# Two transformer layers moved ahead of a diffusion block, with the modulation weights loaded between their dense tiles

## The reference

```python
x = first_block(x, mem, ...)      # layer 0: sink attention + spatial gating unit + cross attention + 16 experts
                                  # layer 1: pooling mixer + cross attention + 16 experts
for i in range(2):                # second_block; last = (i == 1)
    mod  = silu(c)     @ ada_w[i] + ada_b[i]     # sh1, sc1, g1, sh2, sc2, g2 of the latents
    modc = silu(c_ctx) @ ada_w[i] + ada_b[i]     # the same six of the context
    h  = modulate(rmsnorm(x,  norm1_g[i]), sh1, sc1)
    hc = modulate(rmsnorm(xc, norm1_g[i]), csh1, csc1)
    y, yc = diff_attention(h, hc, ...) if i == 0 else gqa_attention(h, hc, ...)   # keys: context and latents
    x = x + g1 * y
    x = x + g2 * swiglu(modulate(rmsnorm(x, norm2_g[i]), sh2, sc2), ffn_w_gu[i], ffn_w_down[i])
    if not last:                  # the context gets its own output only in layer 0
        xc = xc + cg1 * yc
        xc = xc + cg2 * swiglu(modulate(rmsnorm(xc, norm2_g[i]), csh2, csc2), ...)
```

## Time and profile before

| | |
|---|---|
| time, median of 3 runs | 2428.16 us (2425.42 to 2431.86) |
| the profiled execution | 2427.91 us, of which its span 2426.1 us |
| busy in the span | PE 82%, PEld 62%, POOL 41%, DVE 31%, ACT 30% |
| granted clock of TensorE, mean | 0.909 of full speed |
| DMA | 482 MB, mean 199 GB/s |

### The profile page before, as it was taken

One profiled execution on the slowest core, in us unless ns is written; L12 is line 12 of the kernel. 1 busy time (PEld: TensorE's weight loads), 2 busy tenths in 40 slices (PEclk: granted clock), 3 DMA queues, 4 the chain that ended last, 5 costly groups with the idle time before them and its releaser, 6 DMA issues. The chain is left out here.

```text
span 2426.1 us, 29349 instructions
## 1 busy us (share of the span) xinstructions
PE 1992.6 (82%) x11525; PEld 1505.0 (62%) x11525; DVE 754.8 (31%) x1394; ACT 736.7 (30%) x1025; POOL 1003.2 (41%) x784
## 2 busy tenths in 40 slices
PE   5569579998779779996798699976975999787998
PEld 0029469987558644443687444435744999656997
DVE  0113832125443321113232311123784211453112
ACT  0024534443323210002233110012463444354442
POOL 0037048886227200003574000014703788524886
PEclk8879779999769989998999799997987999898999
DMA  8985236655214449997443399994402466312663
GB/s 328 374 290 172 70 108 181 184 191 182 78 52 156 157 174 409 409 409 281 138 160 119 115 410 409 409 366 156 128 12 78 146 186 192 123 52 79 190 180 99
DMA packets 298434, 482.25 MB, mean 199 GB/s; under 512 B 16890, under 2 KB 200172, under 8 KB 297932
## 3 DMA queue, kind: packets, MB, share of 16 engines
q1 hardware_dynamic: 288284, 458.67, 53.4%
q10 hardware_dynamic: 10032, 21.93, 2.7%
HBM read 476.77 MB, written 3.77 MB: 198 GB/s over the span
## 5 line engine op out<-in xcount | busy, mean ns | idle before, releaser
L580 POOL TENSOR_TENSOR w_lo<-raw,w_hi 128x512 fp32r<-128x512 f32 x780 | 1003.0, 1321 | 1404.7 <-ACT w_hi L1276 1404.6
L630 PE MATMUL PS<-at_hi,w_hi 128*128 128x256 f32 x1680 | 492.1, 293 | 33.0 <-DVE at_lo L1786 29.1
L1276 ACT ACTIVATE w_hi<-raw 128x2048 fp32r<-128x2048 f32 x195 | 371.6, 1909 | 384.5 <-PE PS L632 361.0
L631 PE MATMUL PS<-at_lo,w_hi 128*128 128x256 f32 x1680 | 484.5, 288 | 0.0
L632 PE MATMUL PS<-at_hi,w_lo 128*128 128x256 f32 x1680 | 484.3, 288 | 0.0
L630 PEld LDWEIGHTS PS<-at_hi,w_hi 128*128 128x128 f32 x1680 | 332.2, 198 | 41.5 <-DVE at_lo L1786 31.3
L631 PEld LDWEIGHTS PS<-at_lo,w_hi 128*128 128x128 f32 x1680 | 332.0, 198 | 4.2 <-issue 3.1
L632 PEld LDWEIGHTS PS<-at_hi,w_lo 128*128 128x128 f32 x1680 | 331.6, 197 | 0.0
L630 PE MATMUL PS<-w_hi,at_hi 128*128 128x512 f32 (+1 forms) x480 | 192.3, 401 | 56.4 <-DVE at_lo L1786 28.9
L631 PE MATMUL PS<-w_lo,at_hi 128*128 128x512 f32 (+1 forms) x480 | 188.9, 394 | 0.0
L632 PE MATMUL PS<-w_hi,at_lo 128*128 128x512 f32 (+1 forms) x480 | 188.5, 393 | 0.0
(11 more groups left out here) (296 smaller groups left out, 2369.9 us busy)
## 6 DMA issues: line engine op xcount, KB each, us to landing
raw<-ffn_w_gu SPq DMA_DIRECT2D x132, 512.0 KB, 4.9
raw<-ada_w SPq DMA_DIRECT2D x64, 768.0 KB, 6.4
raw<-l_e_gate SPq DMA_DIRECT2D x80, 512.0 KB, 10.8
raw<-ffn_w_down SPq DMA_DIRECT2D x66, 512.0 KB, 4.0
raw<-l_e_up SPq DMA_DIRECT2D x64, 512.0 KB, 8.2
raw<-diff_w_in SPq DMA_DIRECT2D x48, 512.0 KB, 4.7
raw<-l_e_down SPq DMA_DIRECT2D x48, 512.0 KB, 13.8
H<-l_e_down SPq DMA_DIRECT2D x40, 512.0 KB, 12.6
```

The costliest lines, as they stand in the source:

```text
L580: ins = nc.gpsimd.tensor_tensor(w_lo[:, n % RING, part], raw[:, n % RAW, part], w_hi[:, n % RING, part].bitcast(F32), ALU.subtract)
L630: pe.matmul(dst, s_hi, m_hi, start=first, stop=False)
L631: pe.matmul(dst, s_hi, m_lo, start=False, stop=False)
L1276: nc.scalar.activation(w_hi[:, n % RING, :], raw[:, n % RAW, :], ACT.Copy).then_inc(hi_done, 1)
```

## The change

The order becomes: (3) and (4) first, then (2) and the first half of (5) together, then the rest of (5). Three things change with it.

*The modulation* is no longer a stage. Its 64 tiles take slots of `raw` between the 27 dense tiles of layer 0, by two tables: `ADA_BEFORE[n]` is how many of them SP has loaded before dense tile n, `ADA_USED[n]` how many PE has used before it. Further ones are used in the attention loops of layer 0 (`mods(11 + it)` in each step of the first). Both conditionings and both layers now sum up in one bank (bank 7), so the other rotating banks are three instead of four until the experts of layer 0. A tile is loaded by two DMAs of 64 partitions. Memory is written before the experts of layer 0 and read behind them.

*The context* stays on the chip: its rows lie in the second half of `H` (`HC`), its keys and values of the differential attention are not written out.

*Context and latents* take turns in one function, `context_and_latents`, on PE, ACT and DVE, one on `at`, the other on `at2`.

```diff
+ADA_BEFORE = [0, 0, 0, 0, 2, 4, 5, 6, 8, 10, 14, 18, 22, 26, 36, 38, 40, 42, 44, 46, 48, 50, 52, 56, 57, 59, 64, MODS]
+ADA_USED = [0, 0, 0, 0, 3, 5, 7, 12, 16, 20, 24, 34, 36, 38, 40, 42, 44, 46, 48, 52, 54, 55, 56, 62, 63, 64, 64, MODS]
...
+            def slot_wait(s):
+                if RAW <= s < RAW + len(SEQUENCE):
+                    kind, at = SEQUENCE[s - RAW]
+                    sp.wait_ge(ada_used if kind == "ada" else lo_done, at + 1)
...
-            modulation(0, 0, RAW)
+            sp.dma_start(X[:, :, :], A["x"][0].rearrange("(t p) d -> p t d", p=P)).then_inc(input_landed, 16)
+            gemm(A["l0_w_in"], 0, D)
             for dst, src in loads[N_COLIN:]:
                 sp.dma_start(dst, src, allow_slow_non_contiguous=True).then_inc(setup_landed, 16)
-            sp.dma_start(X[:, :, :], A["ctx_2"][0].rearrange("(t p) d -> p t d", p=P)).then_inc(x_landed, 16)
-            modulation(0, RAW, MOD_TILES)
-            modulation(1, 0, MOD_TILES)
...
             def tile_wait():
+                mods(ADA_USED[min(c.get("tile"), LAYER_TILES[0])])
                 pe.wait_ge(lo_done, c.lo(c.get("tile")))
...
+            def context_and_latents():            # PE
+                gemm(2, at=1)                      # context V
+                to_at(HL, wait=False)              # latents
+                heads_t(4, 4, 0, False, at=1)      # context K, Q
+                diff_attention(0)
+                pe.wait_ge(y_freed, c.get("y"))
+                at_wait()
+                gemm(1)                            # latents V, first half
+                to_at(HC, wait=False)              # context behind its attention
+                gemm(1)                            # latents V, second half
+                at_wait()
+                gemm(1, at=1)                      # context output, first half
+                tables(0)
+                gemm(1, at=1)                      # context output, second half
+                heads_t(4, 0, 0, True)             # latents K
+                to_at(rows_q, wait=False)          # context, RMS
+                heads_t(0, 4, 0, True)             # latents Q
+                diff_attention(1)
+                gated(F_FFN // P, at=1, between=HL)   # context feed-forward, latents transposed in it
+                gemm(1)                            # latents output, first half
+                to_at(V[:, 2:4, :], wait=False)    # context, RMS
+                gemm(1)                            # latents output, second half
+                at_wait()
+                gemm(1, 256, at=1)                 # context V of the second attention
+                heads_t(1, 0, 1, False, at=1)      # and its K
+                to_at(HL)                          # latents, RMS
+                gated(F_FFN // P)                  # latents feed-forward
...
                 else:
                     to_at(X)
-                    gemm(2)
+                    columns()                      # the read-back modulation, transposed
+                    gemm(1)
+                    to_at(HL, wait=False)          # context, for its V, K, Q
+                    gemm(1)
```

More of the change, by code:

```diff
@@ L372, in build @@
         bias = A["ada_b_2"].rearrange("l (g n w) -> l n g w", g=4, n=3)
-        for layer in range(2):
-            for _, n, rows in mod_parts:
-                loads.append((mod_sums[layer][rows, :], bias[layer, n]))
+        for layer, _, n, rows in mod_parts:
+            loads.append((mod_sums[rows, :], bias[layer, n]))
         assert len(loads) == N_COLIN + N_SETUP
@@ L460, in moe @@
                 g, u, dw = (A[f"l{layer}_e_{s}"] for s in ("gate", "up", "down"))
-                dense, landed = c.get("tile"), layer * (MOE_TILES // MOE_RING)
+                mods_until(MODS)
+                dense = c.get("tile")
                 at = 0
@@ L603, in _, with mods @@
             c = Count()
+            def mods(end):
+                if 0 == c.get("ada") < end:
+                    pe.wait_ge(wb_freed, 7)
+                while c.get("ada") < end:
+                    a = c.get("ada")
+                    s = ADA_AT[a]
+                    pe.wait_ge(raw_landed[s % RAW], 32 * (s // RAW + 1))
+                    for n in range(3):
+                        ins = pe.matmul(mod_bank[32 * n:32 * n + 16, :], spread_of(a),
+                                        raw[:, s % RAW, n * 512:(n + 1) * 512], start=a == 0, stop=a == MODS - 1)
+                    ins.then_inc(ada_used, 1)
+                    c.add("ada")
             def tile_wait():
+                mods(ADA_USED[min(c.get("tile"), LAYER_TILES[0])])
                 pe.wait_ge(lo_done, c.lo(c.get("tile")))
@@ L764, in gated @@
                 step(True)
+                if between is not None:
+                    to_at(between, wait=False)
                 with pe.Fori(0, loops) as i:
@@ L840, in modulation @@
[L840 to L858, removed]
-            bank = wb_wait()
-            for wide in range(2):
-                ins = pe.matmul(bank[:, 2 * wide:2 * wide + 2], swap[wide][:, :], gains[:, 0, 2 * wide:2 * wide + 2],
-                                start=True, stop=True)
@@ L1378, in gated @@
                 step()
+                if between:
+                    to_at()
                 with act.Fori(0, loops) as i:
@@ L2071, in gated @@
                     step()
-                if early:
-                    dve.wait_ge(x_landed, 32)
-                    for _ in range(NT):
-                        ready(dve.tensor_copy(hs[:, 0, 0:1], hs[:, 0, 0:1]))
-                    to_at()
                 c.add("tile")
@@ L2153, in _ @@
             D1(dve.tensor_reduce(select[:, P:P + 4], ident[:, :].rearrange("p (r g) -> p g r", g=4), AXX, ALU.add))
+            full()
+            freed(dve.tensor_copy(col[:, :], bank()[:, 0:C_ROWS]))
+            dve.wait_ge(input_landed, 16)
+            for _ in range(NT):
+                ready(dve.tensor_copy(hs[:, 0, 0:1], hs[:, 0, 0:1]))
+            to_at()
             for wide in range(2):
```

545 lines of the change are left out of this document (281 added, 264 removed).

## The result

The changed kernel takes **2340.1 us** (median of 4 runs, 2337.9 to 2347.2), beside 2429.6 of the kernel before on the same chip: a ratio of 0.9639, 95% interval 0.9613 to 0.9664. The forecast was 2279, its range 2238 to 2322. The sign is right, the gain is 89 us where 148 were forecast.

What follows compares the result with a forecast made beforehand. PE was taken to set the pace outside the experts and a load-bound first stage of 164.6 us. Terms -144.6 + 40.6 + 8 - 52.2 = -148.2 took the span from 2426.1 to 2277.9; forecast 2279 us, range 2238 to 2322.

Steps and rivals of the forecast that it cites:

- Step 1: Start of the kernel: first dense product at 20 us (bounds 17 and 26) instead of 164.6, -144.6 us.
- Step 2: Modulation tiles put among layer 0's dense tiles and attention loops cost PE time: +40.6 us.
- rival E: Whole kernel: nothing gained, the modulation's 50 MB only displace other loads in layer 0; chance 0.02, including mixtures near no change.
- Dense tiles 7.5 us apart: Expected profile sign in layer 0: dense tiles of `w_out` and `xkv` 7.5 us apart, PE not waiting for `w_lo`.
- Step 3: Layer 1: reading the modulation back, small transposes, context transposes and a copy or two, +8 us (3 to 14).
- Step 4: Context and latents taking turns on the engines fill PE's gaps: -52.2 us (bounds -92 and 0).
- four stretches: Experts to context's K -18 us; context attention to output product -12; to latents' Q -7.6; to latents' feed-forward -14.6.
- The doubt about DVE beside POOL: Two head norms: DVE operations with two SBUF inputs wait for POOL's splits, sum about 8 us higher.
- C: Covers leak: ten DVE chains slowed by POOL, dense tiles late among modulation; +46 us, 2325 us, chance 0.18.
- Its sign: What would show the forecast wrong: sum of DVE waits above 60 us where context and latents take turns.
- D: Ring of four slots runs in series, 17.6 us a dense tile instead of 7.5: +232, 2511 us, chance 0.03.

Runs made afterwards that it cites:

- e4: Changed kernel without any load or slot for modulation tiles, products in full on a constant tile: 2268.7 us.
- e9: Changed kernel, modulation tiles keep slots and waits but load 128 of 1536 columns, products in full on a constant tile: 2288.9 us.
- e1: Changed kernel with each modulation tile loaded as two column halves over all 128 partitions instead of two halves of 64 partitions: 2308.1 us.
- e3: Changed kernel with all loads, but products of 62 of 64 modulation tiles over 16 columns instead of 512: 2335.0 us.
- e6: Changed kernel with ACT splitting the fourth dense tile of the context's V in layer 1 ahead of the latents' squares: 2333.4 us.
- e12: Kernel before the change, each modulation tile loaded as two column halves over 128 partitions instead of one transfer: 2430.0 us, ratio 1.0011.
- e2: Kernel before the change, with each modulation tile loaded as two halves of 64 partitions: 2514.3 us in a single run.

## Why the prediction was wrong

Added up, layer 0 by its windows: 311.3 without modulation, + 26.6 products (e4), + 20.6 order (e9, 358.5), + 21.1 bytes (e1, 379.6), + 33.0 partition halves = 412.6. The medians say much the same: 2239.8, 2268.7, 2288.9, 2308.1, 2340.1. The terms are differences in this order of taking things off; in another order the shares can differ (with late loads the products cost 5 us in e3, without loads 29 in e5).

- **Step 1** was right in mechanism, off by 4.7 us: PE's first dense product came at 24.7 instead of 20, inside its bounds of 17 and 26. ACT's third split ended at 20.7 where the prediction had 16; it waited for its tile.
- **Step 2 failed, at the sentence "The loads keep up by order: a dense tile's slot is freed by a modulation tile used three dense tiles earlier, 3 x 7.5 = 22 us, and load plus split need 12."** The prediction costed what TensorE issues, and took a load at the 4.7 us of the earlier trace rows, measured in a layer that moved 121 GB/s. Three prices are missing from it. They come to 75 us. The products were 12.7 cheaper, 1.3 of lateness was in the forecast already, and the rest of layer 0 took 3.5 more, which leaves the 64.
  - *Partition halves, 33 us.* The prediction gave the halves no term. It compared GB/s with GB/s in rival E (150 more would fit), while the load itself had become 1.7 times as dear in engine time.
  - *Bytes, 21 us.* Even in column halves the engines are at 0.65 in layer 0 (e1), and a dense tile of `l_xkv` took 6.2 us to land, where it took 4.7 in the quiet layer of the earlier trace rows and 4.3 in e4 at a share of 0.32.
  - *Order, 21 us.* The 22 us of slack hold for `w_out` to `xq`, where e9 and e4 differ by nothing. At both ends they don't: the first modulation tiles can't be used before the table is spread, and in the cross attention a dense tile queued behind modulation tiles holds ACT. The prediction had 2 us for the first and none for the second.
  - *Products, 27 us*, where 22.6 + 5 + 3 and the 8.7 of `w_in` make 39: more of them hides than was thought.
- **Dense tiles 7.5 us apart**: true of the first two distances only. The eight dense tiles between the gating unit and the transposes start at 212.4, 219.9, 227.4, 237.6, 248.3, 257.1, 269.4 and 278.8 us; PE waits for modulation tiles in between, not for `w_lo`, as was said. In e4 the same stretch is 66.6 us long instead of 79.6.
- **Step 3** was right to a microsecond. **Step 4** was right to a microsecond in its sum (-51.7 for -52.2), and that was luck: of its four stretches three missed by 6 to 8 us, in both directions. The windows of the changed kernel:

```profile
1201.20:1244.10 42.90, 27.58 (x113) 21.93 (x113) 26.68 (x39) 16.62 (x21) 37.01 (x27) 0.91 0.53 172
1345.50:1395.30 49.80, 46.12 (x214) 38.08 (x213) 25.18 (x31) 17.77 (x15) 37.24 (x29) 1.00 0.46 148
1395.30:1475.30 80.00, 67.06 (x456) 59.64 (x456) 48.07 (x50) 34.02 (x46) 42.92 (x33) 0.89 0.38 116
1538.90:1798.30 259.40, 232.90 (x1563) 215.73 (x1562) 89.97 (x119) 112.98 (x131) 201.56 (x156) 0.96 0.53 162
```

  The forecast had 37.2, 57, 72 and 261.5 us. The first stretch lacks the 6.3 us before the context's K. In the second the four half products took 11.0 to 11.2 us each at a clock of 1.00, not 11.5, the 16 transposes 1.9 instead of 3.7, and the head norm was covered to the end. In the third K and Q took 64.6 us, not 59, and 15.4 lie between them, not 13. The fourth was 2 us shorter than forecast. The experts, the context's K and Q and the two attentions, at 0 in the forecast, gave another -4. The single waits that the prediction named came nearly as written. PE, 1228 to 1800 us:

```profile
PE PS L678 <- DVE at_lo L1838: 8.3, 2, 6.6
PE PS L678 <- POOL w_lo L613: 6.6, 2, 4.4
PE PS L678 <- DVE PB L1958: 6.4, 2, 3.6
PE PS L678 <- DVE V L2005: 6.4, 1, 6.4
```

  4.4 for the fourth tile (forecast 6), 3.6 and 2.9 for the banks of a product (3), 6.4 at `heads_t` (6), and before the latents' feed-forward 6.6 and 4.2, the latter at the transposes (10).
- **The doubt about DVE beside POOL** (8 us at the two head norms) did not come true, because POOL was idle then: it waited for ACT's split,

```profile
1356.98 5.86 POOL L613 TENSOR_TENSOR w_lo<-raw,w_hi 128x512 fp32r<-128x512 f32 x4 [51.50 <-ACT w_hi L1334]
```

  and the norm's large operations, from 1346.37 to 1357.92, took 1.22 to 1.23 us each, as before the change. The place where such an operation was slow is the one under e6.
- **The rivals.** C's 2325 is the nearest number, for another reason: its DVE chains beside POOL would have shown in part 4, which held in its sum. Its sign, waits for DVE above 60 us in part 4, was just met (60.3 us from 953.1 to 1798.3), but 24.4 of them stand inside the attention loops, where the kernel before had 24.0. D named the right place, the ring of four, at ten times its price, and gave it the time of a full series. None of the five lets the transfers themselves become dearer.
- **The range** reached 2322 and left out what was needed: step 2's bounds were built from PE's and the clock's, none from the DMA's.

## What to carry to other kernels

When loads move from a stage of their own into one where they share slots and engines, cost them three times: in bytes, in engine time for a MB in the form in which the new code issues them, and in what stands behind them in the queue and behind the engine that waits for them. A transfer split for another reason was best split along columns here: that cost nothing measurable (e12), while the lower and the upper 64 partitions took 1.7 times the engine time of the whole (e2). An agreement in a sum says little before its parts are compared too, as step 4 shows. To find where such a cost lies, take off one layer at a time (columns, slots, bytes, form): each difference is one term of the sum.

## What was not expected of the hardware

- Two loads of partitions 0 to 63 and 64 to 127 cost 71 us of one DMA engine for a MB, one of all 128 partitions 41, two column halves 42. Even and odd partitions are as quick as column halves, in the share of the queue.
- With loads late, cutting 62 of 64 tiles' products from 512 to 16 columns was worth 5 us of 2340, within the noise: PE waited longer for the loads, and its granted clock in layer 0 was 0.76 (e3) instead of 0.84.
- An operation of DVE with two inputs in SBUF that takes 0.68 us alone took 4.35 beside an unbroken run of POOL's instructions, in one place of one trace.
